# First stage of a fused two-block kernel: new order of the loads, ten of sixteen modulation units on TensorE, first w_in units woven in, context last

## The chip, the cores and the metric

The kernel runs on one core of one Trainium2 chip. The metric is the time on the device in microseconds, the median of a few executions; less is better. All rows below come from one profiled execution.

## The reference

The network is two blocks over 512 latent tokens of width 1024, with 256 context tokens. All is float32. The change lies at the start of the first block, which computes

```
mod_x = silu(c) @ w_mod + b_mod          # six chunks of 1024: shift, scale, gate, ...
mod_c = silu(c_ctx) @ w_mod + b_mod
hx = rms_norm(x,   g_pre_mix) * (1 + sc_m)  + sh_m      # 512 tokens
hc = rms_norm(ctx, g_pre_mix) * (1 + csc_m) + csh_m     # 256 tokens
project(hx, w_in), project(hc, w_in)     # then attention, retention, FFN, second block
```

`sh_m`, `sc_m` are the first two chunks of `mod_x`, `csh_m`, `csc_m` those of `mod_c`. So before the first projection can start, the first 2048 columns of `w_mod` have to be multiplied with two conditioning vectors, and x and the context have to be normalised.

## The kernel before

**Units.** Weights come from HBM in units of 128 output columns (128 x 1024 floats, 512 KB). The sixteen first modulation units are numbered m = 0 to 15: 0 to 7 give the shift of the eight feature tiles, 8 to 15 the scale. A unit is computed in one of two ways. On TensorE (`modulation(m)`, L648): eight feature tiles kt, each a float32 weight load and a matmul of two columns (the latent and the context conditioning vector) into columns 2m, 2m+1 of PSUM bank 7; in the trace a float32 matmul is two records, so a unit is sixteen. On VectorE (`first_modulations(m)`, L1793): the unit is stored transposed and two multiply-and-reduce instructions (one per conditioning vector, against `crow_t`, a conditioning vector repeated on all partitions and passed through Silu on ScalarE, L1180) each give one column of `dert`. `MOD_ORDER` is the order in which the sixteen are loaded, `MOD_ON_PE = 6` sends m < 6 to TensorE, `MOD_ROWS` lists the other ten in VectorE's order. The first four units loaded go to the four slots of `wraw`, the ring that the w_in units use next; the other twelve to `mfirst` buffers, eight of which lie under H.

**Loads.** All are issued by SyncE in program order (L495 to L540): the column constants `colt`, two conditioning rows, the ones matrix, six first units, x in two halves (`X`), seven first units, the context (`Xc`), three first units, three small matrices, then the w_in units. `load_static` waits until the ring's slot has been read.

**Norms.** ScalarE squares one feature tile at a time into a double buffer `sqb` (`square`, L1161), TensorE adds them up over partitions with a matmul against `ones` (`squares_total(k)`, L685, k = 0 for x into bank 6, k = 1 for the context into bank 5), ScalarE makes the inverse root by a logarithm and an exponential (`rstd`, L1189 and L1191; `rstdc`, L1206 and L1208). VectorE multiplies tile by tile with gain and inverse root into `tb` (`scaled`, L1737). ScalarE adds the shift and writes the high part of H (`high`, L1166), VectorE the low part (`low`, L1737): products are split into high and low parts, three matmuls for one. `split_hi` (L596, ScalarE) and `split_lo` (L602, VectorE) do the same for a w_in unit. `tb` has four buffers: tile kt + 4 waits for the low part of tile kt.

**TensorE's order** is written out by hand: modulation 0 to 2, squares of x, modulation 3 to 5, squares of the context, then a loop over the 22 w_in units: latent part (24 matmuls of 512 columns, L613, from H), for the first ten a context part (24 of 256 columns, from Hc), then helpers (`aux`, L708 on, which transposes the first unit's result). The latent part of unit 1 goes ahead of the context part of unit 0.

**VectorE's order**: three row units, small scalings of the decay constants (L1817, L1819), five row units, the gains `a_mix` and `a_ctx` from all eight scale units, `tb` tiles 0 to 3, the last two row units, the sum of TensorE's columns and the bias (L1847), low half of unit 0, low parts of H with `tb` tiles between, low half of unit 1 inside them, then the context's tiles.

**ScalarE's order**: Silu of the column vectors, Silu of the two rows, a table load, three exponentials, squares of x, inverse root, squares of the context with the high half of unit 0 inside, then high parts of H.

## Time and profile before

| what | us |
|---|---|
| runs: median (lowest, highest), 3 of them | 1465.45 (1464.59, 1466.54) |
| span of the profiled execution, first to last instruction | 1463.1 |
| TensorE matmul busy in it | 1407.7 (96%) |
| VectorE busy | 918.3 (63%) |
| ScalarE busy | 534.0 (37%) |
| GpSimd busy | 105.5 (7%) |

The page lists no time of its own for the profiled execution beside the span. PE is TensorE's matmuls, PEld its weight loads, DVE VectorE, ACT ScalarE, SPq the issuing of loads by SyncE. PEclk is the granted share of TensorE's full clock (1.00 is 2.4 GHz, 0.50 is 1.2 GHz). Times in rows are microseconds from the span's start. L613 is line 613 of the kernel.

### The profile page before, as it was taken

What the parts mean: (1) busy time and instruction counts of PE and PEld (TensorE: products, weight loads), DVE (VectorE), ACT (ScalarE), POOL (GpSimd) and SP (SyncE); (2) the same over time, 40 slices, a digit from 0 to 9 for tenths busy, and PEclk for the clock granted to TensorE, in tenths of its full rate; (3) what the DMA queues carried; (4) which work ended last, traced back from release to release, by engine and by line L of the source; (5) the groups of instructions that cost most, each with busy time, mean ns of one, the idle gap of its engine ahead of it and who ended that gap; (6) DMA issues with size and microseconds to landing.
All of it is one profiled execution on the core that took longest, in us unless ns stands there. A gap on an engine that the chain in (4) does not pass through costs nothing.

```text
span 1463.1 us, 16608 instructions
## 1 busy us (share of the span) xinstructions
PE 1407.7 (96%) x6120; PEld 1095.3 (75%) x6120; DVE 918.3 (63%) x1239; ACT 534.0 (37%) x750; POOL 105.5 (7%) x117
## 2 busy tenths in 40 slices
PE   6899999999989999999999899999989999999996
PEld 5688887666758888888885387777867888888885
DVE  6855687784186666663235774989548878876222
ACT  3423353555352232232222553333443333333221
POOL 0002630000200000001110030000110000000010
PEclk9899999999999999999999999999999999999998
DMA  9434330122236666664421022220213222233211
GB/s 375 156 99 144 125 106 9 46 85 88 85 121 228 218 207 227 219 220 148 152 82 44 29 87 72 72 101 29 73 58 101 86 100 100 86 110 120 99 59 58
DMA packets 44801, 169.19 MB, mean 116 GB/s; under 512 B 5547, under 2 KB 6123, under 8 KB 43724
## 3 DMA queue, kind: packets, MB, share of 16 engines
q1 hardware_dynamic: 43340, 165.60, 33.3%
q0 software_dynamic: 1408, 2.89, 0.7%
q8 instruction: 33, 0.54, 0.2%
q14 instruction: 20, 0.16, 0.0%
HBM read 163.49 MB, written 2.10 MB: 113 GB/s over the span
## 4 chain that ended last, share of the span: by engine, by line
PE 88%; DVE 7%; SPq 2%; ACT 1%; DMA 1%; issue 1%; POOL 0%; DVEq 0%; ACTq 0%
PE PS L613 72%; PE PS L998 3%; PE PS L892 2%; PE PS L627 1%; DVE tb L1737 1%; DMA wraw<-w_w_in 1%; PE PS L1117 1%; SPq L505 1%; PE PS L857 1%; PE PS L858 1%; PE PS L754 1%; PE PS L880 1%; PE PS L879 1%; PE PS L816 1%; PE PS L803 1%
## 5 line engine op out<-in xcount | busy, mean ns | idle before, releaser
L613 PE MATMUL PS<-H,wsp 128*128 128x512 f32 x3504 | 810.5, 392 | 6.3 <-DVE wsp L602 3.3
L613 PEld LDWEIGHTS PS<-H,wsp 128*128 128x128 f32 x3504 | 654.5, 188 | 155.2 <-issue 10.2
L602 DVE TENSOR_TENSOR wsp<-wraw,wsp 128x1024 fp32r<-128x1024 f32 (+1 forms) x182 | 236.8, 1302 | 402.7 <-ACT wsp L596 402.3
L596 ACT ACTIVATE wsp<-wraw 128x1024 fp32r<-128x1024 f32 (+1 forms) x182 | 202.7, 1114 | 517.2 <-PE PS L613 507.2
L613 PE MATMUL PS<-hid,wsp 128*128 128x512 f32 x1056 | 240.0, 389 | 0.0
L613 PEld LDWEIGHTS PS<-hid,wsp 128*128 128x128 f32 x1056 | 198.1, 188 | 41.9 <-issue 0.8
L1737 DVE SCALAR_TENSOR_TENSOR cva<-PS,dert,cva 128x441 f32<-128x441 f32 (+2 forms) x176 | 122.2, 695 | 5.5
L1939 DVE CUSTOM_DVE_ANT_0 sink<-mring,crow_t,colt 128x1024 bf16<-128x1024 f32 x56 | 71.7, 1280 | 0.4
L1660 POOL COPY acc<-sqb 128x512 f32<-128x512 f32 x4 | 4.4, 1096 | 784.2 <-ACT sqb L1453 282.6
L1663 POOL TENSOR_TENSOR acc<-acc,sqb 128x512 f32<-128x512 f32 x24 | 41.2, 1718 | 200.4 <-ACT sqb L1638 82.6
L1437 ACT ACTIVATE hid<-hv 128x512 f32 (+1 forms) x22 | 13.9, 632 | 71.3 <-DVE hv L2167 71.3
L2020 DVE TENSOR_REDUCE dert<-PS 128x1 f32<-128x768 f32 x32 | 29.9, 952 | 9.3 <-PE PS L858 9.2
L627 PE MATMUL PS<-H,wsp 128*128 128x512 f32 x96 | 27.4, 446 | 8.6 <-DVE H L1737 8.6
L1737 DVE SCALAR_TENSOR_TENSOR ca<-cb__147,colt,ca 128x512 f32<-128x512 f32 x40 | 33.8, 845 | 2.3 <-ACT ca L1517 1.5
L1617 ACT ACTIVATE sl<-cva,colt 128x512 f32<-128x512 f32 x22 | 15.9, 725 | 51.8 <-DVE cva L1737 51.8
L1683 POOL DMA_DIRECT2D RS<-RU x44 | 21.9, 504 | 172.6 <-ACT RU L1260 136.2
L685 PE MATMUL PS<-sqb,ones 128*128 128x512 f32 (+1 forms) x48 | 26.4, 707 | 7.1 <-ACT sqb L1161 6.9
L627 PEld LDWEIGHTS PS<-H,wsp 128*128 128x128 f32 x96 | 19.8, 216 | 17.1 <-issue 9.3
L1161 ACT ACTIVATE sqb<-X 128x512 f32<-128x512 f32 x32 | 19.9, 627 | 32.9 <-DVE X L1781 14.9
L613 PEld LDWEIGHTS PS<-Hc,wsp 128*128 128x128 f32 x240 | 30.0, 192 | 0.7
L613 PE MATMUL PS<-Hc,wsp 128*128 128x256 f32 x240 | 30.2, 283 | 0.0
L998 PE MATMUL PS<-zN,fwdt 128*128 128x512 f32 x64 | 28.7, 592 | 0.0
(282 smaller groups left out, 1338.3 us busy)
## 6 DMA issues: line engine op xcount, KB each, us to landing
mring<-mod_c SPq DMA_DIRECT2D x56, 512.0 KB, 4.6
wraw<-w_ffn_in SPq DMA_DIRECT2D x44, 512.0 KB, 3.4
wraw<-w_up SPq DMA_DIRECT2D x44, 512.0 KB, 3.2
wraw<-w_hy_in SPq DMA_DIRECT2D x24, 512.0 KB, 3.2
wraw<-w_w_in SPq DMA_DIRECT2D x22, 512.0 KB, 3.3
wraw<-w_ffn_out SPq DMA_DIRECT2D x16, 704.0 KB, 4.1
wraw<-w_down SPq DMA_DIRECT2D x16, 704.0 KB, 4.1
mfirst<-mod_x SPq DMA_DIRECT2D x12, 512.0 KB, 16.7
```

What stands on the lines that cost most here:

```text
L596: nc.scalar.activation(wsp[:, o % 2, 0, 0:n], wraw[:, g % RAW, 0:n], ACT.Copy).then_inc(w_hi, 1)
L602: nc.vector.tensor_tensor(wsp[:, o % 2, 1, 0:n], wraw[:, g % RAW, 0:n], wsp[:, o % 2, 0, 0:n].bitcast(F32), ALU.subtract).then_inc(w_lo, 1)
L613: mm = nc.tensor.matmul(psum, wsp[:, o % 2, a, wk * P:(wk + 1) * P], h[:, b, kt, :], start=first and kt == kts[0] and (a, b) == (0, 0), st ...
L627: mm = nc.tensor.matmul(psums[u], wsp[:, (o + u) % 2, a, kt * P:(kt + 1) * P], h[:, b, kt, :], start=kt == 0 and (a, b) == (0, 0), stop=kt ...
L685: nc.tensor.matmul(PS[:, bank, 0:n], ones[:, :], sqb[:, q % 2, 0:n], start=kt == 0, stop=kt == KT - 1).then_inc(n_acc, 1)
L892: nc.tensor.matmul(out_bank(h), V[:, kt, h % 2 * HD:h % 2 * HD + P], p_tile(v), start=kt == 0, stop=kt == 5).then_inc(a_pv, 1)
L998: mm = nc.tensor.matmul(PS[:, b0 + a, :], fwdt[:, a, mt, f * P:(f + 1) * P], src[:, (a // 2) * 2 + mt, c * 512:(c + 1) * 512], start=mt == ...
L1663: PL.tensor_tensor(acc_of(k), acc_of(k), sqb[:, q % 2, 0:n], ALU.add).then_inc(n_acc, 1)
L1683: ins = pool.dma_start(moved_tile(n)[to:to + HALF, :], RU[of:of + HALF, n % 2, 0:L])
L1737: return VE.scalar_tensor_tensor(out=o, in0=a, scalar=s, in1=b, op0=op0, op1=op1)
L1939: VE.tensor_tensor_reduce((sink_w if m - 16 < MOD_W else sink)[:, :], unit, crow_t[:, which, :], 1.0, bias, ALU.mult, ALU.add, to).then_in ...
L2020: VE.tensor_reduce(der("mx", u), PS[:, b:b + 2, :].rearrange("p a b -> p (a b)")[:, 0:LA], mybir.AxisListType.X, ALU.max).then_inc(a_mx, 1)
```

## The change

- Loads: the ones matrix and x come straight after the column constants, then the conditioning rows, twelve first units, the first w_in unit, the last four first units, the second w_in unit, and the context last.
- Modulation: units 15, 0, 14, 1, 2, 3, 4, 5, 6, 7 on TensorE (in that order), units 8 to 13 on VectorE. The results of TensorE go to bank 7 (m of 8 and more), 4 (0 to 3), 3 (4, 5) and 2 (6, 7), and VectorE adds the bias in four steps: units 14 and 15 before the gains, then 0 to 3, 4 and 5, 6 and 7 (`m_cols` 1, 2, 3).
- ScalarE: the squares of x start before the Silu of the conditioning rows, which are put between them; the context's squares come after the high halves of both first w_in units.
- TensorE: squares of x, six modulation units, then `first_units`: latent tiles 0 and 1 of unit 0, then modulation 4, 5, 6, 7 alternating with latent tiles 2, 3, 4, 5; latent tiles 0 to 5 of unit 1; squares of the context; the remaining latent tiles. The context parts follow as before.
- VectorE: the low half of unit 1 comes after the last of the shift columns.

```diff
...
 MOD_B = 24
 MOD_C = 2 * MODU - 16 - MOD_B
 MRING = 3
-MOD_ORDER = (8, 0, 9, 1, 10, 2, 11, 12, 3, 13, 14, 4, 15, 5, 6, 7)
-MOD_ON_PE = 6
-MOD_ROWS = (8, 9, 10, 11, 12, 13, 14, 15, 6, 7)
+MOD_ORDER = (8, 15, 9, 0, 10, 14, 11, 1, 12, 2, 13, 3, 4, 5, 6, 7)
+MOD_PE = (15, 0, 14, 1, 2, 3, 4, 5, 6, 7)
+MOD_ROWS = (8, 9, 10, 11, 12, 13)
...
             first = 5 * (y // 4) + (0, 2, 3, 4)[y % 4]
             return [k for k in range(first, first + (2 if y % 4 == 0 else 1)) if k < MOD_C]
 
+        def mod_bank(m):
+
+            return 7 if m >= KT else 4 if m < 4 else 3 if m < 6 else 2
+
         def first_unit(x):
 
             return wraw[:, x, 0:U1] if x < RAW else mfirst[x - RAW][:, :]
...
                         sp.wait_ge(w_lo, ordinal + 1)
                     elif name == "w_in":
                         m = MOD_ORDER[ordinal]
-                        if m < MOD_ON_PE:
-                            sp.wait_ge(mod_done, m + 1)
+                        if m in MOD_PE:
+                            sp.wait_ge(mod_done, MOD_PE.index(m) + 1)
                         else:
                             sp.wait_ge(a_md, 2 * (MOD_ROWS.index(m) + 1))
                     else:
...
                         load(name, i, (START[name] + first + u) % RAW, w[name][i * RAW + (first + u)])
 
             sp.dma_start(colt[:, :], cols).then_inc(s_cols, 16)
+            sp.dma_start(ones[:, :], mats[0]).then_inc(s_small, 16)
+            for k0 in (0, KT // 2):
+                sp.dma_start(X[:, k0:k0 + KT // 2, :], xT[:, k0:k0 + KT // 2]).then_inc(s_x, 16)
             for v in range(2):
                 sp.dma_start(crow_t[:, v, :], crow[:, 2 * v]).then_inc(s_crow, 16)
 
...
                 else:
                     sp.dma_start(mfirst[x - RAW][:, :], mod_x[x - RAW]).then_inc(mfirst_on[x - RAW], 16)
 
-            sp.dma_start(ones[:, :], mats[0]).then_inc(s_small, 16)
-            for x in range(6):
+            for x in range(12):
                 load_first(x)
-            for k0 in (0, KT // 2):
-                sp.dma_start(X[:, k0:k0 + KT // 2, :], xT[:, k0:k0 + KT // 2]).then_inc(s_x, 16)
-            for x in range(6, 13):
+            load_static("w_in", 0)
+            for x in range(12, 16):
                 load_first(x)
+            load_static("w_in", 1)
             sp.dma_start(Xc[:, :, :], ctxT).then_inc(s_xc, 16)
-            for x in range(13, 16):
-                load_first(x)
             for j, m in ((1, bones), (2, swap), (3, ident)):
                 sp.dma_start(m[:, :], mats[j]).then_inc(s_small, 16)
             def load_beside(k):
...
                 sp.dma_start(mwin[k % 2][:, :], mod_w[k]).then_inc(mw_on[k % 2], 16)
 
             for i in range(22):
-                load_static("w_in", i)
+                if i >= 2:
+                    load_static("w_in", i)
                 if i in (2, 3):
                     load_beside(i - 2)
                 elif 7 <= i < 5 + MOD_W:
...
                 x = MOD_ORDER.index(m)
                 first_landed(pe, x)
                 for kt in range(KT):
-                    mm = nc.tensor.matmul(PS[:, 7, 2 * m:2 * m + 2], first_unit(x)[:, kt * P:(kt + 1) * P],
+                    mm = nc.tensor.matmul(PS[:, mod_bank(m), 2 * m:2 * m + 2], first_unit(x)[:, kt * P:(kt + 1) * P],
                                           dert[:, DER["silu_c"] + 3 * kt:DER["silu_c"] + 3 * kt + 2],
                                           start=kt == 0, stop=kt == KT - 1)
                 mm.then_inc(mod_done, 1)
...
                                      stop=kt == KT - 1).then_inc(n_acc, 1)
 
             pe.wait_ge(silu_c, 1)
-            for m in range(3):
-                modulation(m)
             pe.wait_ge(s_small, 16)
             squares_total(0)
-            for m in range(3, MOD_ON_PE):
+            for m in MOD_PE[:6]:
                 modulation(m)
-            squares_total(1)
 
             def aux(n):
 
                 if n < NV:
                     pe.wait_ge(q_ev, n + 1)
                     if n == 0:
-                        pe.wait_ge(m_cols, 1)
+                        pe.wait_ge(m_cols, 3)
                     else:
                         pe.wait_ge(v_ev, n)
                     for t in range(LA // P):
...
                                               stop=i > 1 or i == 1 and t == NPAIR - 1)
                 mm.then_inc(g_st, 1)
 
-            def latent_part(n):
-
-                return split_matmuls(pe, ORD["w_in"] + n, PS[:, n % 2, :], H, range(KT), 0, True, True,
+            def latent_part(n, kts=range(KT)):
+
+                return split_matmuls(pe, ORD["w_in"] + n, PS[:, n % 2, :], H, kts, 0, kts[0] == 0, kts[-1] == KT - 1,
                                      (n_h, 0) if n == 0 else None)
 
+            def first_units():
+
+                pe.wait_ge(w_lo, ORD["w_in"] + 1)
+                latent_part(0, (0, 1))
+                modulation(4)
+                latent_part(0, (2,))
+                modulation(5)
+                latent_part(0, (3,))
+                modulation(6)
+                latent_part(0, (4,))
+                modulation(7)
+                latent_part(0, (5,))
+                pe.wait_ge(w_lo, ORD["w_in"] + 2)
+                latent_part(1, range(6))
+                squares_total(1)
+                latent_part(0, (6, 7))
+                latent_part(1, (6, 7))
+
+            first_units()
             for n in range(22):
                 pe.wait_ge(w_lo, ORD["w_in"] + n + 1)
                 if n >= 2:
                     pe.wait_ge(q_ev, n - 1)
-                if n != 1:
                     mm = latent_part(n)
-                if n == 0:
-                    pe.wait_ge(w_lo, ORD["w_in"] + 2)
-                    latent_part(1)
                 if n < NCTX:
                     mm = split_matmuls(pe, ORD["w_in"] + n, PS[:, 2 + n % 2, 0:LC], Hc, range(KT), 0, True, True,
                                        (n_h, KT) if n == 0 else None)
...
 
             act.wait_ge(s_cols, 16)
             SC.activation(der("silu_c", 0, 3 * KT), col("c", 0, 3 * KT), ACT.Silu).then_inc(silu_c, 1)
+            act.wait_ge(s_x, 32)
+            for kt in range(3):
+                square(kt, X[:, kt, :])
             act.wait_ge(s_crow, 32)
-            for v in range(2):
-                SC.activation(crow_t[:, v, :], crow_t[:, v, :], ACT.Silu).then_inc(crow_on, 1)
+            SC.activation(crow_t[:, 0, :], crow_t[:, 0, :], ACT.Silu).then_inc(crow_on, 1)
+            for kt in range(3, 5):
+                square(kt, X[:, kt, :])
+            SC.activation(crow_t[:, 1, :], crow_t[:, 1, :], ACT.Silu).then_inc(crow_on, 1)
+            for kt in range(5, KT):
+                square(kt, X[:, kt, :])
             SC.preload_act_table_set("natural_log_exp_and_others")
             SC.activation(der("lg_f", 0, 8), col("dec_f", 0, 8), ACT.Exp).then_inc(m_lg, 1)
             SC.activation(der("lg_b", 0, 8), col("dec_b", 0, 8), ACT.Exp).then_inc(m_lg, 1)
             SC.activation(der("lg_p", 0, 8), col("dec_p", 0, 8), ACT.Exp).then_inc(m_lg, 1)
-            act.wait_ge(s_x, 32)
-            for kt in range(KT):
-                square(kt, X[:, kt, :])
             act.wait_ge(n_acc, KT)
             SC.activation(rtmp[:, :], PS[:, 6, :], ACT.Ln, bias=col("eps")).then_inc(n_rt, 1)
             act.wait_ge(n_rt, 1)
...
             act.wait_ge(m_arg, 1)
             SC.activation(der("kd", 0, 32), der("kd", 0, 32), ACT.Exp).then_inc(r_kd, 1)
             SC.activation(der("gam", 0, 8), der("lg_p", 0, 8), ACT.Exp, scale=float(P)).then_inc(r_kd, 1)
+            split_hi(act, "w_in", 0)
+            act.wait_ge(m_cols, 1)
+            for kt in range(4):
+                high(0, kt, H[:, 0, kt, :], mod_col(0, kt))
+            act.wait_ge(m_cols, 2)
+            for kt in range(4, 6):
+                high(0, kt, H[:, 0, kt, :], mod_col(0, kt))
+            split_hi(act, "w_in", 1)
             act.wait_ge(s_xc, 16)
             for kt in range(2):
                 square(KT + kt, Xc[:, kt, :], LC)
-            split_hi(act, "w_in", 0)
+            act.wait_ge(m_cols, 3)
+            for kt in range(6, KT):
+                high(0, kt, H[:, 0, kt, :], mod_col(0, kt))
             for kt in range(2, KT):
                 square(KT + kt, Xc[:, kt, :], LC)
-            act.wait_ge(m_cols, 1)
-            for kt in range(4):
-                high(0, kt, H[:, 0, kt, :], mod_col(0, kt))
-            split_hi(act, "w_in", 1)
             act.wait_ge(n_acc, 2 * KT)
             SC.activation(accc[:, :], PS[:, 5, 0:LC], ACT.Ln, bias=col("eps")).then_inc(n_rt, 1)
             act.wait_ge(n_rt, 2)
             SC.activation(rstdc[:, :], accc[:, :], ACT.Exp, scale=-0.5).then_inc(n_rs, 1)
-            for kt in range(4, KT):
-                high(0, kt, H[:, 0, kt, :], mod_col(0, kt))
             for kt in range(KT):
                 high(1, kt, Hc[:, 0, kt, :], mod_col(0, kt, 1), LC)
 
...
                 ins = VE.tensor_scalar(der("kd", 8 * v, 8), der("lg_f" if v < 2 else "lg_b", 0, 8), col("key_pos", v), None,
                                        ALU.mult)
             ins.then_inc(m_arg, 1)
-            for m in MOD_ROWS[3:8]:
+            for m in MOD_ROWS[3:]:
                 first_modulations(m)
 
             def mod_pair(chunk, which):
...
             def mod2_col(chunk, kt):
                 return der("mod2", KT * chunk + kt)
 
-            dve.wait_ge(a_md, 2 * KT)
+            dve.wait_ge(a_md, 2 * len(MOD_ROWS))
+            dve.wait_ge(mod_done, 3)
+            own(VE.tensor_tensor(der("mod", 28, 4), PS[:, 7, 28:32], col("b_mod", 28, 4), ALU.add))
             own(stt(der("a_mix", 0, KT), mod_pair(1, 0), 1.0, col("g_pre_mix", 0, KT), ALU.add, ALU.mult))
             stt(der("a_ctx", 0, KT), mod_pair(1, 1), 1.0, col("g_pre_mix", 0, KT), ALU.add,
                 ALU.mult).then_inc(m_gain, 1)
             dve.wait_ge(m_gain, 1)
             scaled(0, X, "a_mix", (0, 1, 2, 3))
-            for m in MOD_ROWS[8:]:
-                first_modulations(m)
-            dve.wait_ge(a_md, 2 * (16 - MOD_ON_PE))
-            dve.wait_ge(mod_done, MOD_ON_PE)
-            VE.tensor_tensor(der("mod", 0, 2 * MOD_ON_PE), PS[:, 7, 0:2 * MOD_ON_PE], col("b_mod", 0, 2 * MOD_ON_PE),
-                             ALU.add).then_inc(m_cols, 1)
+            def shift_columns(part, first, n):
+
+                dve.wait_ge(mod_done, len(MOD_PE) - 8 + first + n)
+                VE.tensor_tensor(der("mod", 2 * first, 2 * n), PS[:, mod_bank(first), 2 * first:2 * (first + n)],
+                                 col("b_mod", 2 * first, 2 * n), ALU.add).then_inc(m_cols, 1)
+                dve.wait_ge(m_cols, part)
+
+            shift_columns(1, 0, 4)
             split_lo(dve, "w_in", 0)
-            dve.wait_ge(m_cols, 1)
-            lows(0, 0, H, lambda kt: mod_col(0, kt), X, "a_mix", range(0, 5))
+            lows(0, 0, H, lambda kt: mod_col(0, kt), X, "a_mix", range(0, 4))
+            shift_columns(2, 4, 2)
+            lows(0, 0, H, lambda kt: mod_col(0, kt), X, "a_mix", range(4, 6))
+            shift_columns(3, 6, 2)
             split_lo(dve, "w_in", 1)
-            lows(0, 0, H, lambda kt: mod_col(0, kt), X, "a_mix", range(5, KT))
+            lows(0, 0, H, lambda kt: mod_col(0, kt), X, "a_mix", range(6, KT))
             scaled(1, Xc, "a_ctx", (0, 1, 2, 3), LC)
             dve.wait_ge(s_small, 64)
             own(VE.tensor_tensor(centre[:, :], ident[:, :], bones[:, :], ALU.subtract))
...
```

The host lays out first units by the same list (a unit of `MOD_PE` as it is, others transposed).

## Rows read from the trace of the kernel before

**Rows 1.** The page: the chain that ended last, by engine, share of the span

```profile
PE 88%; DVE 7%; SPq 2%; ACT 1%; DMA 1%; issue 1%; POOL 0%; DVEq 0%; ACTq 0%
```

**Rows 2.** Timeline of PE: start us, us, instruction, count [idle before <-releaser]

```profile
10.67 6.96 PE L648 MATMUL PS<-dert,wraw 128*128 128x2 f32 x32 [10.67 <-DMA wraw<-w_mod_a]
17.49 3.55 PE L648 MATMUL PS<-dert,mfirst 128*128 128x2 f32 x16
21.42 9.29 PE L685 MATMUL PS<-sqb,ones 128*128 128x512 f32 x16 [0.38 <-ACT sqb L1161]
30.54 5.85 PE L648 MATMUL PS<-dert,mfirst 128*128 128x2 f32 x48
36.25 2.05 PE L685 MATMUL PS<-sqb,ones 128*128 128x256 f32 x4
40.58 5.34 PE L685 MATMUL PS<-sqb,ones 128*128 128x256 f32 x12 [2.27 <-ACT sqb L1161]
...
48.34 0.97 PE L613 MATMUL PS<-H,wsp 128*128 128x512 f32 x3 [0.27 <-DVE H L1737]
...
53.45 7.79 PE L613 MATMUL PS<-H,wsp 128*128 128x512 f32 x33 [1.48 <-DVE H L1737]
61.08 5.92 PE L613 MATMUL PS<-Hc,wsp 128*128 128x256 f32 x48
66.83 0.82 PE L708 MATMUL PS<-ident,VT 128*128 128x128 f32 x6
```

**Rows 3.** Windows: stretch, us, busy us (instructions) per engine, PEclk, DMA share, GB/s

```profile
40.00:45.00 5.00, 4.42 (x10) 2.80 (x11) 4.75 (x9) 2.66 (x8) 0.00 (x0) 0.50 1.00 396
45.00:50.00 5.00, 3.84 (x13) 2.21 (x13) 4.89 (x8) 4.97 (x9) 0.00 (x0) 0.94 0.34 123
```

**Rows 4.** Timeline of DVE, columns as in rows 2

```profile
9.84 1.29 DVE L1793 CUSTOM_DVE_ANT_0 sink<-wraw,crow_t,colt 128x1024 bf16<-128x1024 f32 x1 [9.84 <-ACT crow_t L1180]
...
17.91 0.58 DVE L1817 TENSOR_SCALAR dert<-dert 128x8 f32<-128x8 f32 x3
...
21.93 1.28 DVE L1793 CUSTOM_DVE_ANT_0 sink<-mfirst,crow_t,colt 128x1024 bf16<-128x1024 f32 x1 [2.77 <-DMA mfirst<-mod_x]
...
35.65 0.37 DVE L1737 SCALAR_TENSOR_TENSOR dert<-dert,colt 128x8 f32<-128x8 f32 x2
36.06 2.74 DVE L1737 SCALAR_TENSOR_TENSOR tb<-X,dert,rstd 128x512 f32<-128x512 f32 x4
...
44.22 1.22 DVE L602 TENSOR_TENSOR wsp<-wraw,wsp 128x1024 fp32r<-128x1024 f32 x1
...
54.64 1.67 DVE L1737 SCALAR_TENSOR_TENSOR tb<-Xc,dert,rstdc 128x256 f32<-128x256 f32 x4
...
60.12 1.27 DVE L1737 SCALAR_TENSOR_TENSOR Hc<-tb,dert,Hc 128x256 fp32r<-128x256 f32 x3
```

**Rows 5.** Windows of L648 (modulation records) alone: PE, PEld, PEclk, DMA, GB/s

```profile
30.60:33.60 3.00, 3.00 (x29) 3.00 (x28) 1.00 1.01 407
35.40:36.20 0.80, 0.80 (x6) 0.80 (x5) 0.50 0.99 369
```

**Rows 6.** Windows of L685 (squares against ones) alone, columns as in rows 5

```profile
21.50:24.90 3.40, 3.40 (x4) 1.35 (x5) 1.00 1.03 410
26.00:30.00 4.00, 4.00 (x10) 1.38 (x10) 1.00 1.04 422
```

**Rows 7.** The page: DMA issues, KB each, us to landing

```profile
mfirst<-mod_x SPq DMA_DIRECT2D x12, 512.0 KB, 16.7
```

**Rows 8.** Timeline of ACT, columns as in rows 2

```profile
7.80 2.00 ACT L1180 ACTIVATE crow_t<-crow_t 128x1024 f32<-128x1024 f32 x2 [3.81 <-DMA crow_t<-crow]
9.82 1.28 ACT L1181 ACT_TABLE_LOAD   x1
...
20.65 1.15 ACT L1161 ACTIVATE sqb<-X 128x512 f32<-128x512 f32 x2 [9.12 <-DMA X<-xT]
...
48.14 0.45 ACT L1206 ACTIVATE accc<-PS,colt 128x256 f32<-128x256 f32 x1
```

More of the change, by code:

```diff
@@ L2555 @@
     rows_a = rows_of(a["w_mod"][0])
-    first = np.stack([mod1[m] if m < MOD_ON_PE else rows_a[m] for m in MOD_ORDER])
+    first = np.stack([mod1[m] if m in MOD_PE else rows_a[m] for m in MOD_ORDER])
     weights = dict(
```

## The prediction

> **What bounds the kernel now.** The page first: TensorE carries 88% of the chain that ended last [rows 1]. Whatever lengthens or shortens its queue moves the end one for one, provided nothing later absorbs it; the chain runs through TensorE without a break from 53.45 us on. The change only touches what lies ahead of that, so I read the first 70 us alone. The measure I use is the moment at which TensorE ends the context part of the second w_in unit: 66.83 us, where the row of the transposes begins [rows 2]. From there both kernels issue the same instructions in the same order.
>
> In the windows VectorE is nearly full, 4.75 and 4.89 of 5 us, while TensorE idles 0.6 and 1.2 us [rows 3]. The engine timelines say why. TensorE does three modulation units, the squares, three more units, then waits for squares and for H tiles; its H matmuls come in threes between gaps [rows 2], since VectorE spends 0.67 us on a tb tile and as much on an H tile. VectorE starts its rows when the second conditioning row is through ScalarE (9.84 us), does ten units of 2.7 us, and is never idle from 21.93 to 61.4 us [rows 4]. So VectorE sets the pace of the first stage, and taking four units from it is a sensible target. TensorE's clock stands at 0.50 from 35.4 to 45 us [rows 3, 5].
>
> **Prices of the parts.** A modulation unit on VectorE: three take 8.15 us (9.84 to the scalings at 17.91), 2.7 us each [rows 4]. Four leave it: 10.9 us. On TensorE a unit is 16 short records (8 tiles, two each). The first 32 take 6.96 us and all 48 of them 10.4 (10.67 to 21.04), one per 0.21 [rows 2]; from 30.6 us 29 stand in 3.0 us, one per 0.11; where the granted clock reads 0.50 they are back at 6 in 0.8 us [rows 5]. So 3.41 us a unit at the 1.2 GHz level and 16 x 0.112 = 1.79 us at 2.4 GHz. The first three show the slow spacing, whatever the clock column reads there, and I go by the spacing. For the squares of X the same doubling: 4 records in 3.4 us, later 10 in 4.0 [rows 6].
>
> What the engine did before the clock fell is the heart of this case. From 30.54 us TensorE ran nothing but modulation records with 2 columns, back to back and 100% busy, and 4.8 us later the clock was at 0.50 [rows 2, 5]. It came back only at 45.6 us, after the context squares had run tightly from 40.58 us. Half-filled stretches (the squares x4 at 36.25, then a gap to 40.58) did not bring it back [rows 2, 3]. The Trainium skill, page "TensorE: Matmul & The Clock Gate", Part 1, ties the clock to how busy TensorE has recently been and warns of idle gaps alone. Read literally, an unbroken modulation stream stays at 2.4 GHz; by that the sum would come out as in the first rival below. The trace disagrees: 100% busy, and the clock fell.
>
> Bytes: the second half-megabyte unit landed by 10.67, the seventh by 21.93, with 2 MB of X between: nine half-megabytes in 11.3 us, 1.25 us each [rows 2, 4, 7]. X now goes ahead of the conditioning rows. These landed at 7.80 [rows 8]; with X (four halves, 5.0 us) and the 64 KB matrix ahead they land at 13.0. X lands 2.5 to 4.0 us before that (two halves at the full rate, or the 4.0 us they took while the loads started up): 9.0 to 10.5, I take 9.7.
>
> **The new stage, step by step.**
> a) Squares of X: ScalarE 0.6, then TensorE from 10.4 us; they took 9.29 us before with the clock rising in them [rows 2]; the same: 19.7.
> b) VectorE's start gets later. Both conditioning rows pass ScalarE between squares: first at 13.0 to 14.0, squares 3 and 4 paced by TensorE to 15.4, second to 16.4 (1.0 us each [rows 8]). VectorE begins at 16.4 instead of 9.84. Three units 8.15: 24.5; decay scalings 1.2 (0.58, and four like them): 25.8; three units: 33.9; gains 0.4 and the new bias sum 0.1; four tb tiles 2.7 [rows 4]: 37.1. Before it stood there at 38.7 with two units still to do, at 44.2 at the low half of unit 0.
> c) TensorE's first six units: fast for 4.8 us (2.7 units), then 3.3 units x 3.41 = 11.3: 35.8.
> d) Shift columns 0.2, low half of unit 0 1.2 [rows 4]: 38.5; first H tile 0.7: 39.2. TensorE idles 3.4 us. All loads are in by then: unit w_in 0 is the thirteenth half-megabyte after 13.0, at about 29.5, and the wait of SyncE ahead of it (VectorE's unit 8, done at 19.1) leaves several issued units in flight, so it costs nothing; four first units, the second w_in unit and the context queue behind it (36 to 39 us), all before their users here.
> e) The weave: tile = 3 matmuls of 0.235 (33 in 7.79 us [rows 2]); at 1.2 GHz 3 x 0.427 = 1.28. No row shows this form at the slow level; the bounds are 0.7 and 1.3, and I take the doubling that both short and wide records show [rows 5, 6]. Two tiles 2.6: 41.8. Then four times (modulation 3.41 + tile 1.28) = 18.8: 60.6. What is woven here, a short wide burst and then a long modulation stream, is nearest to the stretches between 30 and 40 us, which lost the clock or did not regain it, so I leave it slow throughout. VectorE's and ScalarE's part of each tile is done inside the modulation beside it; if a modulation were shorter than that, tile 4 would wait for the second shift columns, 0.2 + 0.6 + 0.7 us.
> f) The low half of unit 1 now stands behind the last shift columns, so behind the last modulation (59.3): 60.9. Eighteen matmuls, dense: the clock rises after 3.7 us (21.42 to about 25.1 [rows 6]) or 5.0 us (40.58 to 45.6 [rows 3]), I take 4.4 us: 10.3 slow, 7.7 fast: 67.1.
> g) Context squares. Before they were done at 45.7, long ahead of their users; now they come after six tiles of unit 1. Fast they have no row: half the pitch of the wide ones (0.47) to the slow 0.86 each; I take 0.5: 4.0 for eight: 71.1.
> h) Logarithm and exponential 0.45 each [rows 8], and only now VectorE can make the context tiles: 6.8 us before, from 54.64 to 61.4 [rows 4]. TensorE has 12 matmuls (2.8 us) to put beside it and then follows tile by tile: last tile at 78.8, its matmuls 0.4, unit 1's context half 24 x 0.123 = 3.0 [rows 2]: 82.1.
> Result 82.1 against 66.8: **15.3 us later**. The moved loads, the 64 KB matrix and the earlier squares cost nothing beyond this; the banks of their own and the later column count ahead of the transposes cost nothing, since each is met long before its reader; nothing behind 67 us waits for VectorE or a load in a way that could take it back.
>
> The page's span is 1463.1; the runs' median 1465.45 stands 2.4 above it, and the page gives no time of its own. The difference goes on the median: 1480.7.
>
> **Rivals.** (1) The clock stays at 2.4 GHz through modulations: c ends at 30.5 and still waits for VectorE to 39.2; e is 1.4 + 4 x 2.5 = 11.4: 50.6; f waits to 51.2, 4.2: 55.4; g 59.4; h 70.5. Slower by 3.7: 1469.1. For it: dense wide matmuls stand between the modulations; against it, the fall at 35.4 [rows 5].
> (2) The relief of VectorE decides, faster. If the clock holds and context squares and context tiles run beside the latent tiles, each engine's work alone counts: TensorE from 10.4: 9.3 + 10 x 1.79 + 48 x 0.235 + 4.0 + 5.9 = 48.4, to 58.8; VectorE from 33.9: 0.5 gains, 2.7 first tb tiles, 0.4 shifts, 2.4 low halves, 8.0 for twelve tb and H tiles, 6.8 context, to 54.7. The end is 8 us earlier: 1457.4. It decides if step h's 7.7 us lie under TensorE's work, and only if no more than some two units run slow (each slow one costs 1.6). Against it: the written order puts h after g.
> (3) Extra table loads: squares now stand between the Silu calls. No row shows a Square right after a Silu, so up to four loads of 1.28 us [rows 8] could appear; start at 16.4 becomes up to 21.5, TensorE's block moves alike: 1485. The Trainium skill, page "ScalarE: Activation LUTs", section "Table sets: the hidden batching unit", says that cheap functions are in every set; no run here shows it for Square.
> (4) It does nothing: gains and losses cancel within 3 us, 1465. Needs a half-slow weave and a covered h.
>
> **Numbers.** Forecast case 0.75, its own range 1475 to 1485.5 (clock phase -2 or +2, X +-0.7, g up to +2.9, a short rise inside the weave -3); rival 1 0.10; rival 2 0.08; rival 3 0.04; rival 4 0.03. The range takes in rival 1 and rival 3: 1468.5 to 1486; what it leaves out are rivals 2 and 4 and the tails, under 2 in 10. About 0.2% (2.9 us) is what can be told from no change here. Slower 0.88, same 0.04 (rival 4 and the near edge of rival 1), faster 0.08.
>
> **What would show it.** Granted clock 0.50 from about 25 to 64 us with TensorE busy; modulation records 0.21 us apart; a gap of some 3 us before the first H matmul near 39; VectorE idle some 7 us ahead of the second shift columns, 6 ahead of the third and 9 before the context tiles; the transposes behind the second w_in unit beginning near 82. Wrong: a clock of 1.00 through the weave (then 70 us), or VectorE starting its rows before 14 us.

## The result, and the profile after

The changed kernel takes 1483.21 us (median of 4 runs, 1479.89 to 1484.42) against 1465.26 us for the kernel before (4 runs): 18.0 us more, ratio 1.0122 with a 95% interval of 1.0110 to 1.0134. It is slower, as forecast; the forecast was 1480.7, 15.3 us more than the median that it started from. The profiled execution took 1483.92 us around a span of 1482.1, 19.0 above the span before. Of these, 18.5 have arisen by the moment at which the transposes behind the second w_in unit begin: 85.31 us against 66.83 [rows 2].

The page's chain that ended last still names TensorE for most of it, as in [rows 1]:

```profile
PE 89%; DVE 8%; ACT 1%; issue 1%; DMA 1%; POOL 0%; SPq 0%; DVEq 0%; ACTq 0%
```

Timeline of TensorE in the changed kernel, columns as in [rows 2]. L690 are squares, L653 modulations, L618 the w_in matmuls:

```profile
12.17 6.77 PE L690 MATMUL PS<-sqb,ones 128*128 128x512 f32 x10 [12.17 <-ACT sqb L1178]
...
22.08 3.63 PE L653 MATMUL PS<-dert,wraw 128*128 128x2 f32 x32
25.57 12.81 PE L653 MATMUL PS<-dert,mfirst 128*128 128x2 f32 x64
41.63 2.90 PE L618 MATMUL PS<-H,wsp 128*128 128x512 f32 x6 [3.25 <-DVE H L1762]
44.33 3.41 PE L653 MATMUL PS<-dert,mfirst 128*128 128x2 f32 x16
...
61.68 8.02 PE L618 MATMUL PS<-H,wsp 128*128 128x512 f32 x21
69.54 4.64 PE L690 MATMUL PS<-sqb,ones 128*128 128x256 f32 x16
73.83 3.08 PE L618 MATMUL PS<-H,wsp 128*128 128x512 f32 x12
77.72 1.72 PE L618 MATMUL PS<-Hc,wsp 128*128 128x256 f32 x9 [0.80 <-DVE Hc L1762]
...
81.19 4.28 PE L618 MATMUL PS<-Hc,wsp 128*128 128x256 f32 x33 [0.17 <-DVE Hc L1762]
85.31 0.82 PE L710 MATMUL PS<-ident,VT 128*128 128x128 f32 x6
```

The first two modulation units take 3.63 us together, the next four 12.81. At 1.79 us a fast unit and 3.41 a slow one, those four are slow from about the middle of their first on. Each unit of the weave takes 3.41 us. The context squares, done at 45.9 us before [rows 2], begin at 69.54, and the context part of unit 0 then goes in pieces behind VectorE.

Windows of the changed kernel, columns as in [rows 3]:

```profile
0.00:5.00 5.00, 0.00 (x0) 0.00 (x0) 0.00 (x0) 1.51 (x2) 0.20 (x4) 1.00 0.62 176
5.00:10.00 5.00, 0.00 (x0) 0.00 (x0) 0.00 (x0) 0.00 (x0) 0.00 (x0) 1.00 0.99 408
...
20.00:25.00 5.00, 5.00 (x32) 3.59 (x32) 4.64 (x9) 3.52 (x7) 0.00 (x0) 1.00 1.03 412
25.00:30.00 5.00, 5.00 (x33) 5.00 (x32) 4.82 (x14) 0.33 (x2) 0.00 (x0) 0.67 1.03 410
30.00:35.00 5.00, 5.00 (x25) 5.00 (x25) 4.64 (x9) 1.06 (x1) 0.00 (x0) 0.50 1.03 411
...
45.00:50.00 5.00, 5.00 (x22) 4.71 (x22) 0.46 (x1) 0.00 (x0) 0.00 (x0) 0.50 0.24 95
...
65.00:70.00 5.00, 5.00 (x18) 3.99 (x18) 0.00 (x0) 0.00 (x0) 0.00 (x0) 0.74 0.21 79
```

TensorE is 100% busy from 25 to 35 us and from 45 to 50, and its granted clock still falls to 0.50. The mean of 0.67 from 25 to 30 us puts the fall at about 26.7, the 0.74 from 65 to 70 puts the rise at about 67.6, and every stretch between them reads 0.50. In the kernel before it was low for 10 us [rows 3, 5], here for about 41.

Timelines of VectorE, as [rows 4], and of ScalarE, as [rows 8]:

```profile
18.74 1.28 DVE L1818 CUSTOM_DVE_ANT_0 sink<-wraw,crow_t,colt 128x1024 bf16<-128x1024 f32 x1 [18.74 <-ACT crow_t L1202]
...
39.41 0.16 DVE L1873 TENSOR_TENSOR dert<-PS,colt 128x8 f32<-128x8 f32 x1
...
52.47 0.16 DVE L1873 TENSOR_TENSOR dert<-PS,colt 128x4 f32<-128x4 f32 x1 [7.01 <-PE PS L653]
...
61.86 0.16 DVE L1873 TENSOR_TENSOR dert<-PS,colt 128x4 f32<-128x4 f32 x1 [6.29 <-PE PS L653]
...
75.18 1.67 DVE L1762 SCALAR_TENSOR_TENSOR tb<-Xc,dert,rstdc 128x256 f32<-128x256 f32 x4 [10.58 <-ACT rstdc L1235]
```

```profile
11.40 1.15 ACT L1178 ACTIVATE sqb<-X 128x512 f32<-128x512 f32 x2 [7.31 <-DMA X<-xT]
...
14.79 1.04 ACT L1199 ACTIVATE crow_t<-crow_t 128x1024 f32<-128x1024 f32 x1
...
74.73 0.42 ACT L1235 ACTIVATE rstdc<-accc 128x256 f32<-128x256 f32 x1
```

VectorE begins its rows at 18.74 instead of 9.84 and has three new waits: 7.01 us for modulation 5, 6.29 for modulation 7, 10.58 for the context's inverse root. Before, it had none from 21.93 to 61.4. No table load has appeared between the squares and the Silu calls: the Silu at 14.79 follows the square of 14.25 (0.63 us) directly.

### The profile page after: what moved, and what is told of

Its sections match the earlier page's. It is cut to its first block, busy times and chain, and to the rows that moved or that the text cites. A ratio compares the mean times of both kernels' runs of the same rounds, so it can differ in the third digit from the quotient of the medians.

```text
span 1482.1 us, 16723 instructions
## 1 busy us (share of the span) xinstructions
PE 1425.5 (96%) x6184; PEld 1113.1 (75%) x6184; DVE 908.6 (61%) x1226; ACT 534.1 (36%) x750; POOL 105.8 (7%) x117
## 4 chain that ended last, share of the span: by engine, by line
PE 89%; DVE 8%; ACT 1%; issue 1%; DMA 1%; POOL 0%; SPq 0%; DVEq 0%; ACTq 0%
PE PS L618 71%; PE PS L1015 3%; PE PS L909 2%; PE PS L632 2%; DVE tb L1762 1%; PE PS L1134 1%; DVE sink L1818 1%; PE PS L653 1%; PE PS L690 1%; PE PS L874 1%; PE PS L875 1%; DMA X<-xT 1%; PE PS L897 1%; PE PS L896 1%; PE PS L756 1%
## 5 line engine op out<-in xcount | busy, mean ns | idle before, releaser
L618 PE MATMUL PS<-H,wsp 128*128 128x512 f32 x3504 | 817.1, 394 | 6.6 <-DVE wsp L607 3.3
L618 PEld LDWEIGHTS PS<-H,wsp 128*128 128x128 f32 x3504 | 658.4, 189 | 154.8 <-issue 10.2
L618 PE MATMUL PS<-hid,wsp 128*128 128x512 f32 x1056 | 240.0, 389 | 0.0
L618 PEld LDWEIGHTS PS<-hid,wsp 128*128 128x128 f32 x1056 | 198.1, 188 | 41.9 <-issue 0.8
L690 PE MATMUL PS<-sqb,ones 128*128 128x512 f32 (+1 forms) x48 | 23.7, 630 | 17.3 <-ACT sqb L1178 17.0
L1183 ACT ACTIVATE H<-tb,dert 128x512 fp32r<-128x512 f32 x32 | 22.1, 720 | 40.1 <-DVE dert L1873 24.9
L618 PE MATMUL PS<-Hc,wsp 128*128 128x256 f32 x240 | 31.4, 285 | 1.5 <-DVE Hc L1762 1.3
L618 PEld LDWEIGHTS PS<-Hc,wsp 128*128 128x128 f32 x240 | 30.2, 191 | 3.3 <-DVE Hc L1762 1.5
L690 PEld LDWEIGHTS PS<-sqb,ones 128*128 128x128 f32 x48 | 8.9, 213 | 31.2 <-issue 19.3
```

The lines of the kernel that those rows point to most:

```text
L618: mm = nc.tensor.matmul(psum, wsp[:, o % 2, a, wk * P:(wk + 1) * P], h[:, b, kt, :], start=first and kt == kts[0] and (a, b) == (0, 0), st ...
L690: nc.tensor.matmul(PS[:, bank, 0:n], ones[:, :], sqb[:, q % 2, 0:n], start=kt == 0, stop=kt == KT - 1).then_inc(n_acc, 1)
```

## The experiments

Two theories were on the table. Mine: three separate costs, (a) TensorE's clock, lost in long streams of 2-column modulations, (b) the context squares behind unit 1, which lay the whole context chain bare, (c) VectorE's late start, for the most part hidden as long as (a) lasts. Against it: the order alone (who waits for whom), with slow records only as a symptom; or the loads. In every run below the work behind the transposes took between 1395.0 and 1398.0 us in its profiled execution, so a shift of the transposes in a trace carries to the end only to within some 1.5 us.

**e1: hold the clock, change nothing else.** The two conditioning columns are streamed 64 times over.

```diff
...
-                    mm = nc.tensor.matmul(PS[:, mod_bank(m), 2 * m:2 * m + 2], first_unit(x)[:, kt * P:(kt + 1) * P],
-                                          dert[:, DER["silu_c"] + 3 * kt:DER["silu_c"] + 3 * kt + 2],
+                    mm = nc.tensor.matmul(mod_slot(m), first_unit(x)[:, kt * P:(kt + 1) * P],
+                                          dert[:, DER["silu_c"] + 3 * kt:DER["silu_c"] + 3 * kt + 2]
+                                          .unsqueeze(1).to_broadcast([P, 64, 2]),
                                           start=kt == 0, stop=kt == KT - 1)
...
```

`mod_slot(m)` is a place of 128 columns in the same bank; VectorE reads its first two columns.

> The changed kernel; only the modulation matmuls on TensorE differ: the two conditioning columns are repeated 64 times, so each streams 128 columns into a PSUM place of its own (same results, the first two columns are read). Clock theory: the wide stream keeps TensorE at 2.4 GHz, records stay 0.11 us apart also beyond 5 us of modulation, granted clock 1.00 from about 20 us on, six units end near 33 instead of 38.4, the weave of four units takes 4 x 2.5 instead of 4 x 4.7 us, the transposes begin near 75 instead of 85.3: 9 to 10 us faster than the changed kernel, about 1473 us, still 7 to 9 slower than before (VectorE's late start and the context chain behind the squares remain). Rival, order theory: the time is lost in who waits for whom, and the slow records are only what a waiting engine shows: no more than 2 us faster. Rival, cost of streaming: 128 columns instead of 2 make each record longer, no gain or slower.

Measured: 1472.46 us, ratio to before 1.0051 (1.0034 to 1.0068); 10.8 us of the loss are gone. Windows of the modulation line alone (L667), columns as in [rows 5], one window of all engines, columns as in [rows 3], and the timeline of TensorE:

```profile
22.00:25.00 3.00, 3.00 (x30) 3.00 (x29) 1.00 1.02 408
25.00:31.00 6.00, 6.00 (x56) 6.00 (x55) 1.00 1.04 411
```

```profile
35.00:40.00 5.00, 0.00 (x0) 0.00 (x0) 4.83 (x11) 1.08 (x2) 0.00 (x0) 0.63 1.05 350
```

```profile
24.98 7.31 PE L667 MATMUL PS<-dert,mfirst 128*128 128x128 f32 x64
40.95 2.90 PE L632 MATMUL PS<-H,wsp 128*128 128x512 f32 x6 [8.66 <-DVE H L1777]
...
47.50 1.95 PE L667 MATMUL PS<-dert,mfirst 128*128 128x128 f32 x16
...
75.94 0.82 PE L725 MATMUL PS<-ident,VT 128*128 128x128 f32 x6
```

Thirty records fit into 3 us, as many as with 2 columns at the same clock (29 [rows 5]): the 126 further columns cost nothing here. The weight loads come at the same spacing, 0.11 us (29 in those 3 us), which would explain it; no run varies them by themselves. The four units behind 24.98 take 7.31 us instead of 12.81, and in the weave a unit and a tile together take 2.48 us (47.50 to 49.98 in this trace) instead of 4.69 (44.33 to 49.02). All six units are done at 32.3 and TensorE then idles 8.66 us, because VectorE is not ready: cost (c) has come out from under (a). In that gap the clock fell to 0.50 as well (0.63 from 35 to 40 us); 40.95 shows two tiles at 2.90 us, the slow time. So the clock was not held throughout.

**g1: the control.** e1 also moved the results in PSUM. Here they are in e1's places with 2 columns streamed.

The matmul against the changed kernel's:

```diff
...
-                    mm = nc.tensor.matmul(PS[:, mod_bank(m), 2 * m:2 * m + 2], first_unit(x)[:, kt * P:(kt + 1) * P],
+                    mm = nc.tensor.matmul(mod_results(m, 1)[:, 0, :], first_unit(x)[:, kt * P:(kt + 1) * P],
                                           dert[:, DER["silu_c"] + 3 * kt:DER["silu_c"] + 3 * kt + 2],
...
```

`mod_results(m, 1)[:, 0, :]` is the first two columns of `mod_slot(m)`; VectorE reads as in e1.

> Control for e1, which changed two things at once: the modulation results in places 128 columns apart, and the streamed width. Here the places are e1's and the width is 2 columns as in the changed kernel. Clock theory: the width alone did it, so the time is the changed kernel's, 1480 to 1485 us, granted clock 0.50 through the weave. Rival (the places in PSUM or the way VectorE reads them gave the gain): e1's 1472 us.

Measured: 1484.54 us, ratio 1.0129 (1.0114 to 1.0144), the changed kernel's time. Window:

```profile
55.00:60.00 5.00, 5.00 (x21) 4.61 (x21) 2.08 (x3) 2.37 (x5) 0.00 (x0) 0.50 0.01 2
```

Clock 0.50 at 100% busy. Of the two things that e1 changed, the width did it.

**e2: the context squares early.** TensorE sums them behind latent tiles 0 and 1; ScalarE makes squares and inverse root before high parts 4 and 5.

```diff
...
     latent_part(0, (0, 1))
+    squares_total(1)
     modulation(4)
...
     latent_part(1, range(6))
-    squares_total(1)
     latent_part(0, (6, 7))
```

> The changed kernel; only the context squares move: TensorE adds them up behind latent tiles 0 and 1 of unit 0 (before modulation 4), ScalarE makes them and the context's inverse root before the high parts 4 and 5. Context-chain theory: the gap between the last latent matmul and the transposes closes, since root, inverse and context tiles no longer stand behind six tiles of unit 1; transposes near 79.5 instead of 85.3, 5 to 6 us faster, about 1477.5 us, if the clock stays slow through the weave as before. If the dense squares raise the clock in passing, a further 1 to 3 us. Rival (only the clock counts): squares cost the same wherever they stand, less than 1.5 us faster.

Measured: 1476.04 us, ratio 1.0072 (1.0055 to 1.0089): 7.2 us less than the changed kernel. Timeline of TensorE:

```profile
44.25 5.76 PE L690 MATMUL PS<-sqb,ones 128*128 128x256 f32 x16
49.84 1.84 PE L653 MATMUL PS<-dert,mfirst 128*128 128x2 f32 x16
...
58.77 1.63 PE L618 MATMUL PS<-H,wsp 128*128 128x512 f32 x3
...
63.47 9.95 PE L618 MATMUL PS<-H,wsp 128*128 128x512 f32 x33
73.25 5.92 PE L618 MATMUL PS<-Hc,wsp 128*128 128x256 f32 x48
79.00 0.82 PE L710 MATMUL PS<-ident,VT 128*128 128x128 f32 x6
```

From 63.47 to 79.00 there is no gap: 33 matmuls of H and 48 of Hc in one run. The clock came back during the squares at 44.25: modulation 4 (49.84) takes 1.84 us; the one before 58.77 was slow again. Of the 6.3 us by which the transposes come earlier, 2.6 are the bared chain (h of the forecast): from the last H matmul's end to the transposes it is 5.8 us instead of 8.4. The other 3.7 stand in the weave with the squares (24.3 to 21.9) and in the 33 H matmuls (10.9 to 9.8), where TensorE is busy almost throughout in both kernels: they are clock. So the clock has the larger part of this gain too.

**e3: both.** The edits of e1 and e2 together in the changed kernel.

> e1 and e2 together in the changed kernel. The sum of both theories: TensorE at 2.4 GHz from 20 us on and the context chain covered; transposes near 72.5, 12 to 13 us faster than the changed kernel, 1470 to 1471 us, still 5 slower than before, because VectorE begins its rows at 18.7 instead of 9.8 us and the first H tile cannot come before 41. If the two gains were the same time counted twice, it would equal the better of e1 and e2.

Measured: 1471.13 us, ratio 1.0040 (1.0026 to 1.0054), as expected, and 1.3 us better than e1 alone. The gains (10.8 and 7.2) do not add up to 18: more than half of e2's was clock, which e1 for the most part holds already. What e2's edit adds on top of e1 is known only roughly, since e1's and e3's times overlap: 1.3 us by the medians, but in the traces the transposes come 3.9 us earlier (75.94 to 72.00), 0.6 of them from the first H matmul. Much of what is left stands in front of the first H tile:

```profile
40.34 2.90 PE L632 MATMUL PS<-H,wsp 128*128 128x512 f32 x6 [8.66 <-DVE H L1775]
...
72.00 0.82 PE L725 MATMUL PS<-ident,VT 128*128 128x128 f32 x6
```

**e4: the conditioning rows first again,** in the loads and on ScalarE, in the changed kernel. The part in the loads:

```diff
...
             sp.dma_start(colt[:, :], cols).then_inc(s_cols, 16)
+            for v in range(2):
+                sp.dma_start(crow_t[:, v, :], crow[:, 2 * v]).then_inc(s_crow, 16)
             sp.dma_start(ones[:, :], mats[0]).then_inc(s_small, 16)
             for k0 in (0, KT // 2):
                 sp.dma_start(X[:, k0:k0 + KT // 2, :], xT[:, k0:k0 + KT // 2]).then_inc(s_x, 16)
-            for v in range(2):
-                sp.dma_start(crow_t[:, v, :], crow[:, 2 * v]).then_inc(s_crow, 16)
...
```

> The changed kernel; only the conditioning rows come first again, in the loads (before the ones matrix and X) and on ScalarE (both Silu before the squares). VectorE starts near 9.9 instead of 18.7 us. Theory: TensorE's six units behind the squares set the first H tile, not VectorE, because X lands 2.5 us later: six units end near 41, first H matmul near 43 instead of 41.6; time within 1.5 us of the changed kernel, 1482 to 1485 us. Rival (VectorE's late start is what costs): 6 to 9 us faster, 1474 to 1477.

Measured: 1484.01 us (1477.53 to 1486.66), ratio 1.0125 (1.0093 to 1.0158): no gain that these runs can show, as the theory wanted; they spread over 9 us, so the interval leaves room for one of some 4 us. But the numbers on the way were off. Timeline of VectorE:

```profile
13.89 1.28 DVE L1814 CUSTOM_DVE_ANT_0 sink<-wraw,crow_t,colt 128x1024 bf16<-128x1024 f32 x1 [13.89 <-DMA wraw<-w_mod_a]
...
33.41 2.74 DVE L1758 SCALAR_TENSOR_TENSOR tb<-X,dert,rstd 128x512 f32<-128x512 f32 x4
38.37 0.17 DVE L1869 TENSOR_TENSOR dert<-PS,colt 128x8 f32<-128x8 f32 x1 [2.22 <-PE PS L653]
```

It starts at 13.89 and not near 9.9: the rows are there, but its first unit now lands behind X. TensorE's six units end at 38.3, not near 41, and the first H matmul comes at 40.61, not near 43: 1.0 us earlier than in the changed kernel. VectorE was ready for the shift columns at 36.1 and waited 2.22 us for TensorE's slow units. In the changed kernel it was the other way round, by 1.0 us. So (c) was real, and all but about 1 us of it was hidden under (a).

**e5: e3 with e4's edit on top.**

> e3 (wide modulations and early context squares) with e4's change on top: conditioning rows first again. With the clock held, TensorE's six units end near 33 and VectorE, starting at 9.9 instead of 18.1, is ready at about 34 to 37, so the same edit that did nothing in e4 now pays: first H tile near 38.5 instead of 40.3, transposes near 68 to 69 instead of 72.0, 2 to 4 us faster than e3, about 1468 us, 2 to 3 above before. Rival (what is left over before is the loads: X and w_in land later whatever comes first): equal to e3 within 1 us.

Measured: 1468.09 us, ratio 1.0022 (1.0012 to 1.0031): the edit that showed nothing in e4 brings 3.0 us here by the medians (the intervals of e3 and e5 just overlap), 2.6 in the traces. Timeline of TensorE:

```profile
38.34 2.90 PE L632 MATMUL PS<-H,wsp 128*128 128x512 f32 x6 [4.68 <-DVE H L1771]
...
69.42 0.82 PE L725 MATMUL PS<-ident,VT 128*128 128x128 f32 x6
```

First H tile at 38.34 instead of 40.34, transposes at 69.42 instead of 72.00. VectorE starts at 14.07 us in this trace, again not at the 9.9 expected. The three edits together take the 18.0 us down to 2.8, read as e1 10.8, e2 on top 1.3, rows first on top 3.0; what the last 2.8 consist of was not tested. The order of taking them off decides what each is worth.

**e6: e1's width in the kernel before.** The same diff as e1's on `modulation`.

> The kernel before; only its modulation matmuls stream 128 columns as in e1. Theory: the clock no longer falls at 35 us, the context squares run in half the time, and nothing comes of it, because VectorE sets the pace up to 61.4 us: within 1 us of before. Rival (the low clock costs wherever it stands): 2 to 4 us faster.

Measured: 1464.69 us, ratio 0.9994 (0.9985 to 1.0003): no difference that can be told. TensorE:

```profile
35.60 1.03 PE L698 MATMUL PS<-sqb,ones 128*128 128x256 f32 x4
...
46.23 5.51 PE L625 MATMUL PS<-H,wsp 128*128 128x512 f32 x15 [1.55 <-DVE H L1750]
...
66.64 0.82 PE L721 MATMUL PS<-ident,VT 128*128 128x128 f32 x6
```

The three modulation units are done and the context squares begin at 35.60 instead of 36.25, and the first H matmul, which waits for VectorE in both kernels, comes at 46.23 instead of 46.44. But the clock did not stay up as expected. Windows of TensorE: stretch, us, busy us (matmuls), PEclk, DMA share, GB/s:

```profile
40.00:45.00 5.00, 4.68 (x12) 0.69 1.01 401
45.00:50.00 5.00, 3.77 (x10) 0.66 0.36 124
```

With 0.96 from 35 to 40 us that makes some 7 us at 0.50, where it had been 10, partly in other places. So e6 shows that the wide stream gains nothing where VectorE sets the pace; that all ten slow microseconds of the kernel before are free, it did not test.

**f1, g2 and f2: a version from the findings.** From the kernel before: two more units go to TensorE (0 to 7), with e1's width, six of the eight (2 to 7) in one block behind the squares of X; five units are loaded ahead of X, the context and the first two w_in units behind all sixteen, and the context squares one by one between the latent tiles, where TensorE waits for VectorE in any case.

```diff
...
-MOD_ORDER = (8, 0, 9, 1, 10, 2, 11, 12, 3, 13, 14, 4, 15, 5, 6, 7)
-MOD_ON_PE = 6
+MOD_ORDER = (8, 0, 9, 1, 10, 11, 2, 12, 3, 13, 4, 14, 5, 15, 6, 7)
+MOD_ON_PE = 8
...
-    squares_total(1)
+    squares_total(1, (0, 1))
...
+    for kt in range(KT):
+        latent_part(0, (kt,))
+        if kt + 2 < KT:
+            squares_total(1, (kt + 2,))
...
```

> A version meant to beat both, made from the kernel before: units 0 to 7 on TensorE, 8 to 15 on VectorE, conditioning rows first, five units ahead of X, context and w_in 0, 1 behind the sixteen units; modulation in one block behind the squares of X, with 128 columns each; context squares one by one between the latent tiles, where TensorE waits for VectorE anyway. Theory: VectorE loses two units (5.4 us) and gets no new wait, the clock stays up; transposes near 62 instead of 66.8, 4 to 5 us faster than before, about 1460.5 us. Rival: TensorE's block of six units or the late context becomes the bound and nothing is gained.

> f1 once more, in other executions, since its runs spread from 1458.2 to 1464.1 us: the interval against before should again lie wholly below 1, near 0.997.

> f1 with modulations of 2 columns again. Clock theory: the block of six units loses the clock after about 5 us, its last three and a half units and the first latent tiles run slow, the shift columns come some 6 us later; transposes near 69, 6 to 8 us slower than f1 and 1 to 3 us slower than before, about 1467.5 us. Rival (order alone makes f1 fast): equal to f1 within 1 us.

Measured: f1 1460.54 us, ratio 0.9966 (0.9954 to 0.9977); the same kernel again (g2) 1461.53 us, 0.9982 (0.9972 to 0.9992). It beats both kernels, by 3.7 to 4.7 us in the medians against the one before; how much of that holds from one set of executions to the next is not settled, since the second interval barely overlaps the first and missed the 0.997 expected. One thing was not as expected: VectorE has a new wait, 2.50 us for TensorE's block of six units (at 39.75 in f1's trace). f2, with 2 columns, took 1470.44 us, 1.0031 (1.0021 to 1.0042): 9.9 us more than f1, where 6 to 8 were expected. Its runs spread from 1466.3 to 1472.8, and the profiled one (1466.99) is among the short ones. TensorE in f1 and in f2:

```profile
28.77 10.88 PE L661 MATMUL PS<-dert,mfirst 128*128 128x128 f32 x96
...
41.93 0.93 PE L626 MATMUL PS<-H,wsp 128*128 128x512 f32 x3 [1.42 <-DVE H L1754]
...
62.80 0.82 PE L722 MATMUL PS<-ident,VT 128*128 128x128 f32 x6
```

```profile
29.08 15.90 PE L649 MATMUL PS<-dert,mfirst 128*128 128x2 f32 x96
...
47.20 1.62 PE L614 MATMUL PS<-H,wsp 128*128 128x512 f32 x3 [0.31 <-DVE H L1741]
...
69.87 0.82 PE L709 MATMUL PS<-ident,VT 128*128 128x128 f32 x6
```

One and the same list of 96 records takes 10.88 us or 15.90, and the transposes come at 62.80 or 69.87. With the narrow stream this order is slower than the kernel before; with the wide one it is faster.

## Why the prediction was right

**a, X and the squares.** The second half of X landed at 11.4, not 9.7: the real landing lies outside my bounds of 9.0 to 10.5. Those bounds took the loads as landing strictly one after the other. The windows give 176 GB/s for the first 5 us, 408 for the next 5 and 419 from there on, so 3.5 MB had moved by 11.4 us, while X and what was issued ahead of it are 2.5 MB: a megabyte of the loads issued behind X had moved beside it. e4, with a further megabyte ahead of X, has X only 1.1 us later (12.49). The landing also differs between executions: 10.50 to 11.69 us in the five traces with this order of loads. TensorE's squares took 9.9 (12.17 to 22.1) instead of 9.3.

**b, VectorE's start.** Forecast 16.4, measured 18.74: 1.7 us from the landing, the rest because ScalarE's squares ahead of the second conditioning row waited for TensorE's slow matmuls. This, not TensorE's block, set the first H tile: the chain of waits runs through VectorE's rows here. The block was done at 38.4 (forecast 35.8), 1.0 us before VectorE asked for it.

**c and e, the clock.** It fell 4 to 5 us after the modulations began and stayed down through the weave. A unit and a tile together take 4.69 us, as priced (3.41 and 1.28). That this meets to the hundredth is luck: from start to start the unit took 3.27 and the tile 1.42. From the first H matmul to the start of the unit-1 run it took 21.7 us (41.63 to 63.3), the forecast 21.7 (39.2 to 60.9). The e1 run against g1 and f1 against f2, each pair in one and the same order, show that this is the clock and that the streamed width decides it.

**f, g, h.** From start to start, the dense run took 6.2 us (6.2), the eight squares 4.3 (4.0; their fast pitch, for which no row stood, is 0.54 instead of 0.5), from there to the transposes 11.5 (11.0). The waits of VectorE came as forecast too: some 7, 6 and 9 us were named, 7.01, 6.29 and 10.58 measured. e2 shows that part of h was a bared chain, 2.6 us.

**The sum.** 85.3 against 82.1 forecast: 2.4 us of the 3.2 stand before the first H tile, 1.7 of them from the landing of X (the mis-sized term of step a) and 0.7 from the pacing in step b; 0.3 come from the squares and 0.5 from the chain behind them. So the sign and the mechanism held and the size was 2.7 us short of 18.0.

**The rivals.** Rival 1 (the clock stays) did not happen, but e1 comes near to that case: 1472.5, where 1469.1 was given. In the traces the gap at the transposes is 5.4 us (75.94 against 70.5): 1.7 from the first H matmul (40.95 against 39.2), and 2.6 because TensorE came back from its 8.66 us of idling at the slow level, which the rival had not foreseen. Rival 2 needed a covered h and a held clock; e3 has the first and, but for the stretch around the first H tiles, the second, and is still 5.9 us slower than before. Its work-only sum left out the waits: TensorE alone waits 8.66 us for the first H tile. Rival 3's table loads did not appear: the Trainium skill, page "ScalarE: Activation LUTs", section "Table sets: the hidden batching unit", says that cheap functions are in every set, without naming Square among them; the trace shows it for Square beside Silu.

On the clock, the page "TensorE: Matmul & The Clock Gate" of the Trainium skill ("Part 1: The HAM clock gate") speaks of how busy TensorE has been. Here it was at 100% both in g1 from 55 to 60 us, at 0.50, and in e1 from 25 to 31 us, at 1.00. The busy share that the profile shows does not tell the two apart.

## What to carry to other kernels

Work that moves to TensorE has to be priced at the clock that it will leave behind. Here the streams of 2-column matmuls left the low one, however busy the engine looked: a unit that seemed to cost 1.8 us cost 3.4, and slowed its neighbours. Where the records of a narrow stream are spaced like their weight loads, try streaming more columns: here it was free and held the clock. When squares, roots or other starters of a chain are moved behind bulk work, look for who only starts then; and taking one cost off (e4) can show little until the one that hides it is gone (e5).

## What was not expected of the hardware

- Float32 records with 128 moving columns follow each other as fast as those with 2: 30 in 3.0 us against 29, 0.11 us each.
- Idle time ahead of the weave cost the clock too: in e1 TensorE came back from 8.66 us of idling at the slow level, two tiles in 2.90 us.
- The loads behind X did not wait for it: when its second half landed, at 11.4 us, 3.5 MB had moved, and only 2.5 MB had been issued up to X.
- The runs of one kernel differ in their mean granted clock, and the longer ones mostly show the lower one: 1459.84 us at 0.989 and 1465.97 at 0.983 (g2), 1466.30 at 0.985 and 1472.77 at 0.980 (f2), 1479.89 at 0.976 and 1484.42 at 0.974 (changed). So TensorE is slow for a different length of time from one execution to the next; what decides it was not tested. It spreads the narrow f2 (6.5 us) and the wide g2 (6.1) alike, against 3.8 for the kernel before.
